# A paged-attention stage in one kernel: the first four value pages loaded right behind the first four key pages

## The reference, cut to what matters

```python
proj = h @ lw['w_in']                      # z, xBC, dt, q, k, v
k_past = cache_k[l][page_table]            # 8 sequences x 8 pages
v_past = cache_v[l][page_table]
z = einsum('bhqd,bhkd->bhqk', q, k) * d ** -0.5 + bias
log_1m = where(mask, log_sigmoid(-z), 0)
tail = cumsum(log_1m, reverse=True) - log_1m
w = where(mask, exp(log_sigmoid(z) + tail), 0)      # stick-breaking weights
o = einsum('bhqk,bhkd->bhqd', w, v)
out = concatenate([y_ssd, o]) @ lw['w_out']
# then norm, gate, ConvFFN (w_ffn_in, depthwise conv, silu, w_ffn_out)
```

## Time and profile before

| what | value |
|---|---|
| median of 3 runs | 1916.65 us (1913.53 to 1919.34) |
| the profiled execution's own time | 1918.85 us |
| its span, first to last instruction | 1916.4 us |
| PE busy | 1735.9 us, 91% of the span |
| DVE, ACT, POOL busy | 1013.8, 665.9, 57.5 us |
| read from and written to device memory | 377.03 MB and 10.41 MB |
| mean granted PE clock | 0.933 |

### The profile page before, as it was taken

One profiled execution on the slowest core, in us unless ns is written; L12 is line 12 of the kernel. 1 busy time (PEld: TensorE's weight loads), 2 busy tenths in 40 slices (PEclk: granted clock), 3 DMA queues, 4 the chain that ended last, 5 costly groups with the idle time before them and its releaser, 6 DMA issues.

```text
span 1916.4 us, 32049 instructions
## 1 busy us (share of the span) xinstructions
PE 1735.9 (91%) x13881; PEld 1553.0 (81%) x13881; DVE 1013.8 (53%) x1329; ACT 665.9 (35%) x663; POOL 57.5 (3%) x153
## 2 busy tenths in 40 slices
PE   5888989998678868989995999999999999999997
PEld 3767878887466645647973999999999999999996
DVE  2334454554657423544546556656556466565566
ACT  3333221222733432124235343333333333333344
POOL 3000000000000000010000000000000000000000
PEclk9889999999889975688995999999999999999999
DMA  9677796888368972046881445454545454545441
GB/s 342 242 245 281 245 334 246 313 312 302 114 224 327 392 280 88 12 143 231 279 285 48 158 163 168 161 169 160 170 157 173 157 173 156 174 156 175 155 153 67
DMA packets 183077, 389.50 MB, mean 203 GB/s; under 512 B 7635, under 2 KB 16067, under 8 KB 182641
## 3 DMA queue, kind: packets, MB, share of 16 engines
q1 hardware_dynamic: 179488, 375.68, 56.4%
q0 software_dynamic: 2752, 9.24, 1.4%
q10 hardware_dynamic: 698, 2.55, 0.4%
HBM read 377.03 MB, written 10.41 MB: 202 GB/s over the span
## 4 chain that ended last, share of the span: by engine, by line
PE 79%; DVE 7%; DMA 5%; ACT 4%; issue 2%; SPq 2%; DVEq 0%; ACTq 0%
PE ps L783 14%; PE ps L781 14%; PE ps L782 14%; PE ps L762 6%; PE ps L763 6%; PE ps L764 6%; PE ps L703 4%; PE ps L742 3%; PE ps L963 1%; SPq L449 1%; DMA kring<-in_cache_k_dram 1%; PE ps L1109 1%; DVE wlo L1696 1%; PE ps L1100 1%; PE ps L996 1%
## 5 line engine op out<-in xcount | busy, mean ns | idle before, releaser
L1696 DVE TENSOR_TENSOR wlo<-raw,whi 128x2048 fp32r<-128x2048 f32 x146 | 332.9, 2288 | 206.1 <-ACT whi L1359 204.5
L1359 ACT ACTIVATE whi<-raw 128x2048 fp32r<-128x2048 f32 x145 | 277.6, 1916 | 449.1 <-PE ps L783 372.5
L781 PE MATMUL ps<-h2hi,whi 128*128 128x288 f32 x1408 | 417.2, 296 | 9.5 <-DVE h2lo L1765 8.7
L783 PE MATMUL ps<-h2hi,wlo 128*128 128x288 f32 x1408 | 420.3, 298 | 0.0
L782 PE MATMUL ps<-h2lo,whi 128*128 128x288 f32 x1408 | 416.8, 296 | 0.0
L781 PEld LDWEIGHTS ps<-h2hi,whi 128*128 128x128 f32 x1408 | 265.3, 188 | 10.5 <-DVE h2lo L1765 9.5
L782 PEld LDWEIGHTS ps<-h2lo,whi 128*128 128x128 f32 x1408 | 266.8, 189 | 0.0
L783 PEld LDWEIGHTS ps<-h2hi,wlo 128*128 128x128 f32 x1408 | 265.2, 188 | 0.0
L762 PE MATMUL ps<-hhi,whi_in 128*128 128x288 f32 x704 | 209.8, 298 | 7.7 <-DVE wlo L1696 7.1
L763 PE MATMUL ps<-hlo,whi_in 128*128 128x288 f32 x704 | 209.3, 297 | 0.0
L764 PE MATMUL ps<-hhi,wlo 128*128 128x288 f32 x704 | 209.2, 297 | 0.0
(11 more groups left out here) (429 smaller groups left out, 2399.4 us busy)
## 6 DMA issues: line engine op xcount, KB each, us to landing
raw<-in_w_ffn_in_dram SPq DMA_DIRECT2D x88, 1024.0 KB, 5.0
raw<-in_w_ada_dram SPq DMA_DIRECT2D x84, 1024.0 KB, 8.4
raw<-in_w_in_dram SPq DMA_DIRECT2D x44, 1024.0 KB, 5.4
raw<-in_w_ffn_out_dram SPq DMA_DIRECT2D x44, 1024.0 KB, 5.0
kring<-in_cache_k_dram SPq DMA_DIRECT2D x64, 512.0 KB, 6.0
vring<-in_cache_v_dram SPq DMA_DIRECT2D x64, 512.0 KB, 5.8
raw<-in_w_out_dram SPq DMA_DIRECT2D x14, 1024.0 KB, 7.5
araw<-in_w_ada_dram SPq DMA_DIRECT2D x8, 1024.0 KB, 18.6
```

What stands on the lines that cost most here:

```text
L781: mm(o, high[:, q, cols], xh, start=(first and q == 0), stop=False)
L783: i = mm(o, low[:, q, cols], xh, start=False, stop=(last and q == QC - 1))
L1359: fn(high_of(g), landed_at(u), ACT.Copy).then_inc(hi_ready, 1)
L1696: tt(low_of(u), landed_at(u), high_of(g).bitcast(F32), SUB).then_inc(lo_ready, 1)
```

## The change

SP's loop is changed in one place. Value pages 0 to 3 are issued in slot 3, right behind key page 3. From slot 13 to 16, where they stood, nothing takes their place, and value page 4 stands in slot 17 as before. No other engine's instructions change.

```diff
@@ -486,7 +486,10 @@
             for n in range(NPAGES + LAG):
                 if n < NPAGES:
                     k_page(n)
-                if n >= LAG:
+                if n == 3:
+                    for v in range(4):
+                        v_page(v)
+                if n >= LAG + 4:
                     v_page(n - LAG)
```

## The result

The change made the kernel a little slower. In the timing that came with the result it took 1926.14 us (median of 20 runs, 1918.21 to 1931.13) against 1918.32 us for the kernel before (20 runs): ratio 1.0036, 95% interval 1.0025 to 1.0047, which is 6.9 us. I timed the same file three more times beside the experiments: 1.0017 (1.0002 to 1.0032), 1.0025 (1.0008 to 1.0042) and 1.0044 (1.0027 to 1.0061). Over all 56 runs of the changed kernel the mean is 1923.59 us, over the 125 runs of the kernel before that were timed beside them and the other experiments 1917.72 us. The difference is 5.9 us, 0.31%. A small loss was forecast, 3.4 us. The measured loss is larger: the first timing lies above the bound of 0.3%, and the runs taken together lie just at it.

A forecast was written before the change was run, and what follows sets the result against it. PE, busy 91% of the span, was taken to bound the kernel, though no single engine bounds the attention stage. 0 + 0 + 2.6 + 0.8 = 3.4 us on the median of 1916.65 us gave 1920.0 us, range 1913.5 to 1925.

The forecast's parts named there:

- Removed transfers: Slots 13 to 16: nothing waits for the four value pages there, so taking them out is worth 0.
- SP's issues ahead of key page 4: SP, slot 3: four issues of about 1.11 us each stay hidden, with 0.3 us to spare.
- The bytes ahead of it: DMA engines: 2.10 MB land key page 4 4.5 us later; less 1.9 us slack, PE's transposes begin 2.6 us later.
- The clock: PE, slot 4: the low level lasts 3.3 us past the restart and adds 0.8 us, bounds 0 and 3.3.
- Carried to the end: From slot 5 on: nothing gives the delay back, so the 3.4 us stay to the end.
- The median of before: Whole kernel: the base of 1916.65 us to which the loss was added, giving 1920.0 us.
- Hidden altogether: Rival, slot 4: key page 4 lands by 474.2, so no loss, 1916.7 us; chance 0.24.
- Double: Rival, slot 4: key page 4 3.2 us late plus 3.3 us of low clock, 6.5 us, 1923.2; chance 0.16.
- Faster by a better place of the pauses: Rival, prompt's attention: seven places come out at full clock, saving 6.6 us, 1913.4; chance 0.08.

The follow-up runs named there:

- late7: The changed kernel with value pages 0 to 3 issued behind key page 7 instead of key page 3: ratio 1.0001 to the kernel before.
- late4: The changed kernel with value pages 0 to 3 issued behind key page 4 instead of key page 3: ratio 1.0001 to the kernel before.
- r_before: The kernel before, unedited, profiled and timed once more beside itself: ratio 1.0006.
- r_after3: The changed kernel, unedited, profiled and timed again: median 1926.94 us, ratio 1.0044 to the kernel before.
- r_after2: The changed kernel, unedited, profiled and timed again: median 1921.50 us, ratio 1.0025 to the kernel before.
- a_warm: The changed kernel with PE kept busy by unread products, two in slot 3 and five in slot 4: ratio 1.0031 to the kernel before.
- three3: The changed kernel with only three value pages behind key page 3, value page 3 back in slot 16: ratio 0.9997 to the kernel before.
- r_after: The changed kernel, unedited, profiled and timed once more for a second profile: ratio 1.0017 to the kernel before.
- b_k4late: The kernel before with no value page moved, only key page 4 held back on SP until tail(0) is done: ratio 1.0029.

## Why the prediction was wrong

The direction, the place and the mechanism were right. Two terms of the sum were too small, and the measured time went above the top of my range: the delay of the transfer, where I had credited 0.6 us of free room that did not exist, and the low clock, 0.8 us forecast and 1.8 measured in the first pair of traces.

*Removed transfers, 0 us.* Right: late7 and late4 keep slots 13 to 16 empty and are as fast as before. Slots 13 to 17 did get shorter in the first pair of traces (from copy to copy 11.9 instead of 13.4 us), but the second traces have it the other way round: 11.9 in r_before, 13.4 in r_after3.

*SP's issues ahead of key page 4, hidden with 0.3 us to spare.* Right in effect. I took 1.11 us for each. The first trace shows more, r_after2 does not (SP's timelines of the two):

```profile
456.12 3.71 SPq L478 DMA_DIRECT2D kring<-in_cache_k_dram  x4
460.60 4.22 SPq L484 DMA_DIRECT2D vring<-in_cache_v_dram  x4
```

```profile
454.80 3.71 SPq L478 DMA_DIRECT2D kring<-in_cache_k_dram  x4
459.28 3.76 SPq L484 DMA_DIRECT2D vring<-in_cache_v_dram  x4
463.99 5.78 SPq L478 DMA_DIRECT2D kring<-in_cache_k_dram  x4
```

From first to last row of the four value pages that is (4.22 - 0.34) / 3 = 1.29 us for each in the first trace and (3.76 - 0.34) / 3 = 1.14 in r_after2. Key page 4 went out 465.92 - 458.45 = 7.5 us behind ACT's first copy in the first, and 463.99 - 457.13 = 6.9 us behind it in r_after2, which is where it stood before (464.90 - 458.04 = 6.9). It landed no earlier for it: 12.9 us after its issue, at 19.8 us, against 19.5 in the first trace. So SP's issues did not set the landing.

*The bytes ahead of it, 4.5 us.* The mechanism was right and the size too small. The landing moved from 14.25 to 19.52 us behind ACT's first copy, by 5.3, where 5.1 us of bytes less 0.6 us of room had been forecast. The room was not there. I had read 289 GB/s in 462 to 464 us as free capacity. But SP's queue was not empty then even before: key page 3, issued at 459.07, took 7.1 us to land. In the changed kernel two, later three of the value pages stood behind it, and the same window moved no more:

```profile
462.00:464.00 2.00, 2.00 (x19) 1.66 (x16) 1.48 (x2) 1.68 (x3) 1.09 (x3) 1.00 0.92 270
```

The DMA engines' share rose from 0.72 to 0.92 without more bytes. Over the first six microseconds behind ACT's first copy the rate was 297 and 327 GB/s in the two traces of the kernel before, and 302, 301 and 315 in after, r_after2 and r_after3. Without the 0.6 us the forecast delay is 5.1, the upper bound that I had written down. The dose of two and three pages and the run without outputs bear out that the traffic ahead of the page makes it late. The start moved from 16.2 to 19.6 us, 3.4 instead of 2.6.

*The clock, 0.8 us.* This step failed by more. I carried the low level's length past PE's restart over from the trace of before, 3.3 us behind `tail(0)`'s start. In the changed kernel PE restarts at 478.01 and the low level lasts to 483.6, 5.6 us; the three other traces put its end 4 to 5 us past the restart. All of `scores(3)` and `tail(1)` and a part of `scores_of(0)` (2.28 instead of 1.93 us) run slowly, and the stretch from start to copy takes 7.3 instead of 5.5 us: 1.8 us where I had 0.8. In the other three traces the stretch takes 6.6 to 7.0 us. a_warm, which keeps the full level throughout, puts the clock's part of slot 4 at 1.8 to 2.3 us. I had written down 3.3 us as its upper bound and had put it into a rival of 0.16, where it and the transfer's bound had to come together; the truth lay between.

*Carried to the end.* Right on average, as far as it can be seen; not in each trace. All times here are behind ACT's second copy. At the end of the stage the four traces of the changed kernel stand at 251.4 to 262.8 us, in the mean 257.5, and the eight kernels that kept slot 4's old start or (three3) nearly so at 252.1 to 254.9, in the mean 253.9. That is 3.6 us, against 4.5 lost in slot 4. r_after kept none of its loss to the end of the stage (251.4), r_after3 stood 9 us late there (262.8); what does this is not shown. The pooled difference of the totals, 5.9 us, is larger than the mean loss of slot 4. That the change shifts the odds of the two paces below is an open rival for the rest: the six traces with a late key page 4 (the four of the change, a_warm, b_k4late) have the slow pace four times, the other eight three times, which decides nothing.

*The median of before.* I added to 1916.65 us, a median of three; that of the later 20 runs is 1918.32. This moved the target by 1.7 us. 1918.32 + 5.2 is 1923.5; the 1926.14 of the first timing holds 2.6 us more. I can't assign these: r_after2 and r_after3 show that two timings of one file differ by more than that. What sets the pace of one execution is open, and so is whether the change shifts the odds of it.

*The rivals.* Hidden altogether: excluded by every trace. Double: the low level did reach into `scores_of(0)`, as its condition said, but only in part; slot 4 lost 5.2 us, not 6.5. Faster by a better place of the pauses: r_after did end its stage as early as the kernels without a loss, but the mean over four traces did not. No version of mine beats the kernel before; late4 and late7 equal it.

## What to carry to other kernels

A transfer that nobody waits for gains nothing by an earlier place, and can cost: look at what stands behind the new place on the queue, how much slack that has (here 1.9 us), and what else fills the DMA engines then (here the outputs). One place further back, behind the last urgent load, the same early loads are free. A window that moves fewer bytes than the fullest one is not free room: here 289 GB/s at a share of 0.72 took up none of the 2.10 MB that were put in front. Where a stall is added to PE, price the low clock behind it as a part of its own, with a range, and don't carry its length over from a shorter pause: here 3.3 us of low level past the restart became 4 to 5.6.

## What the runs showed that I had not expected

**Two paces of the same matmuls.** In the steady feed-forward part, with PE busy all the time and the clock at 1.00, twelve weight units take 76.80 us in 7 traces and 77.44 us in the other 7, 0.83% more, constant within a trace and nothing in between. It does not follow the kernel: four traces of one file show two of each.

**The queues' turns.** At 466 to 468 us of the trace of before, POOL's queue had all of the engines, with key page 4 issued at 464.90, and I read this as a queue that is served first. In the changed kernel, with a backlog on both queues, each had half (52.6% and 50.6%). The rule of the Trainium skill ("DMA: Bandwidth & Descriptors", section "Queues, rings and completion order"), that the engines take turns between queues with work, agrees with this row of the changed kernel. The row of before remains unexplained. In late4 too, key page 4 was issued at 465.72 onto a queue that had run empty, and in the whole of 466 to 469 us nothing of SP's queue moved, while POOL's had 102.1% of the engines. In b_k4late, where the outputs were done, the page issued at 474.11 already moved 0.17 MB in 475 to 476 us. So a new transfer took some 3 us or more to begin beside the full output queue and about 1 us without it. Whether that is a slow start or a form of preference, no run here tells. By the forecast's own argument, that everything in front has to be moved either way, it made no difference to the sum.
